# Banded attention on one core: scores normalised a unit ahead and head by head, biased scores placed between the pieces of the low parts

## The reference, cut to what matters

```python
def chunk_band_attention(qc, kb, vb, key_valid, rel_bias, offset):
    rel = offset + jnp.arange(nq)[:, None] - jnp.arange(nk)[None, :]
    bias = rel_bias[:, jnp.clip(rel, -REL_CLIP, REL_CLIP) + REL_CLIP]
    s = jnp.einsum('bnqhd,bnkhd->bnhqk', qc, kb) * (HEAD_DIM_B ** -0.5) + bias[None, None]
    s = jnp.where(key_valid[None, :, None, None, :], s, NEG)
    p = jax.nn.softmax(s, axis=-1)
    return jnp.einsum('bnhqk,bnkhd->bnqhd', p, vb)
```

## Time and profile before

| what | value |
|---|---|
| three timed runs | 1681.31, 1684.39 and 1684.91 us, median 1684.39 us |
| the profiled execution | 1680.23 us, of it a span of 1678.5 us, mean granted clock 0.973 |
| PE (matmuls) busy | 1585.2 us, 94% of the span |
| VectorE (DVE) busy | 1012.9 us, 60% |
| ScalarE (ACT) busy | 653.5 us, 39% |
| GpSimd (POOL) busy | 305.2 us, 18% |
| band stage | from about 395 us to 572 us of the span |

### The profile page before, as it was taken

The page is one execution under the profiler, slowest core; times in us unless marked ns, Lnnn a source line. Parts: engine busy times, 40 slices in busy tenths (PEclk is TensorE's granted clock), DMA queues, the critical chain, the costliest instruction groups (busy, mean ns, idle before and its releaser), DMA issues.

```text
span 1678.5 us, 27557 instructions
## 1 busy us (share of the span) xinstructions
PE 1585.2 (94%) x11172; PEld 1545.9 (92%) x11172; DVE 1012.9 (60%) x1481; ACT 653.5 (39%) x1146; POOL 305.2 (18%) x354
## 2 busy tenths in 40 slices
PE   6999999997888899999779999999999999999999
PEld 6999999995777799998669999999999999999999
DVE  6625876536888754225653477666666658656653
ACT  5521021126787632214552253333333433333332
POOL 1011000002221010000430004444444421010110
PEclk8999999987999999999999999999999999999999
DMA  7424111002110043201042214433334586454563
GB/s 241 143 89 159 50 39 38 26 1 92 36 37 33 26 138 138 89 26 51 1 148 100 90 55 152 147 143 141 142 142 166 202 281 235 123 165 147 155 211 114
DMA packets 63667, 189.36 MB, mean 113 GB/s; under 512 B 7873, under 2 KB 13049, under 8 KB 63409
## 3 DMA queue, kind: packets, MB, share of 16 engines
q1 hardware_dynamic: 37904, 91.11, 17.1%
q0 software_dynamic: 25648, 96.65, 16.0%
HBM read 138.58 MB, written 54.12 MB: 115 GB/s over the span
## 4 chain that ended last, share of the span: by engine, by line
PE 81%; DVE 7%; ACT 5%; DMA 4%; issue 3%; POOL 1%; SPq 0%; ACTq 0%; DVEq 0%; POOLq 0%
PE ps L452 33%; PE ps L2605 19%; PE ps L2626 17%; PE ps L2163 3%; PE ps L481 2%; DMA a<-wdn 2%; PE ps L2504 2%; PE ps L2356 1%; ACT scores L1168 1%; PE ps L2334 1%; DVE pt_lo L1759 1%; PE ps L2472 1%; PE ps L503 1%; PE ps L2318 1%; DVE scores L1738 1%
## 5 line engine op out<-in xcount | busy, mean ns | idle before, releaser
L452 PE MATMUL ps<-A_hi,w_hi 128*128 128x364 f32 x768 | 174.0, 335 | 0.0
L452 PE MATMUL ps<-A_lo,w_hi 128*128 128x364 f32 x768 | 171.1, 331 | 0.0
L452 PE MATMUL ps<-A_hi,w_lo 128*128 128x364 f32 x768 | 170.7, 331 | 0.0
L393 DVE TENSOR_TENSOR w_lo<-w_raw,w_hi 128x1024 fp32r<-128x1024 f32 x43 | 52.5, 1223 | 150.0 <-ACT w_hi L389 149.6
L389 ACT ACTIVATE w_hi<-w_raw 128x1024 fp32r<-128x1024 f32 x42 | 44.3, 1057 | 241.7 <-PE ps L452 136.2
L452 PEld LDWEIGHTS ps<-A_lo,w_hi 128*128 128x128 f32 x768 | 135.1, 190 | 0.0
L452 PEld LDWEIGHTS ps<-A_hi,w_lo 128*128 128x128 f32 x768 | 135.0, 190 | 0.0
L452 PEld LDWEIGHTS ps<-A_hi,w_hi 128*128 128x128 f32 x768 | 134.2, 191 | 0.0
L2605 PE MATMUL ps<-t_hi,wq_hi 128*128 128x272 f32 x480 | 99.9, 290 | 2.3 <-DVE hid_stage L2059 2.3
L2605 PE MATMUL ps<-t_lo,wq_hi 128*128 128x272 f32 x480 | 99.9, 290 | 0.0
L2605 PE MATMUL ps<-t_hi,wq_lo 128*128 128x272 f32 x480 | 99.7, 289 | 0.0
(11 more groups left out here) (342 smaller groups left out, 4087.6 us busy)
## 6 DMA issues: line engine op xcount, KB each, us to landing
w_raw<-slabs SPq DMA_DIRECT2D x68, 512.0 KB, 4.0
quads_d<-quad_sum POOLq DMA_DIRECT2D x64, 272.0 KB, 2.9
w_raw<-wdn POOLq DMA_DIRECT2D x32, 512.0 KB, 4.0
r_raw_a<-quads_d SPq DMA_DIRECT2D x56, 272.0 KB, 3.1
r_raw_b<-quads_d SPq DMA_DIRECT2D x56, 272.0 KB, 3.0
quads_d<-hid_stage POOLq DMA_DIRECT2D x48, 272.0 KB, 2.9
Y<-xT POOLq DMA_DIRECT2D x16, 546.0 KB, 4.6
y_d<-Y POOLq DMA_DIRECT2D x16, 546.0 KB, 3.2
```

Source lines behind the costliest of these rows:

```text
L393: e.tensor_tensor(WL[:, par], RAW[:, par], WH[:, par].bitcast(F32), ALU.subtract).then_inc(s.w_lo, 1)
L452: ins = e.matmul(PS[:, 3 * par + c, 0:CH], wt[:, wpar, w], xt[:, col:col + CH], start=(first and n == 0 and m == 0), stop=(last and n == l ...
```

## The change

Four orders and two waits are altered; the arithmetic is the same but that the two reciprocals of a unit, one instruction of two columns before, are two instructions of one column now. TensorE issues S(n+2) ahead of V(n-1). ScalarE runs E two units ahead, not one. VectorE does N(n+1) first, then the first two pieces of L(n), then B(n+2), then the rest of L(n).

```diff
                     if n >= 2:
-                        e.wait_ge(s.rec_done, n - 1)
+                        e.wait_ge(s.rec_done, 2 * n - 2)
...
             exps(0)
+            exps(1)
             for n in range(N_U):
                 pt_hi(n)
-                if n + 1 < N_U:
-                    exps(n + 1)
+                if n + 2 < N_U:
+                    exps(n + 2)
...
-                e.wait_ge(s.exp_done, 2 * n + 2)
-                if n >= 2:
-                    e.wait_ge(s.p_ready, 2 * n - 2)
-                e.reciprocal(REC[:, m:m + 2], SUM[:, m:m + 2]).then_inc(s.rec_done, 1)
-                e.wait_ge(s.rec_done, n + 1)
                 for h in range(2):
+                    e.wait_ge(s.exp_done, 2 * n + h + 1)
+                    if n >= 2:
+                        e.wait_ge(s.p_ready, 2 * n - 3 + h)
+                    e.reciprocal(REC[:, m + h:m + h + 1], SUM[:, m + h:m + h + 1]).then_inc(s.rec_done, 1)
+                    e.wait_ge(s.rec_done, 2 * n + h + 1)
...
             biased(0)
+            biased(1)
             normalise(0)
             for n in range(N_U):
                 if n + 1 < N_U:
-                    biased(n + 1)
-                pt_lo(n)
-                if n + 1 < N_U:
                     normalise(n + 1)
+                early = min(2, pieces(n))
+                pt_lo(n, range(early))
+                if n + 2 < N_U:
+                    biased(n + 2)
+                pt_lo(n, range(early, pieces(n)))
...
                 transposes(n)
+                if n + 2 < N_U:
+                    scores(n + 2)
...
                 if n:
                     values(n - 1)
-                if n + 2 < N_U:
-                    scores(n + 2)
```

More of the change, by code:

```diff
@@ L1745, in normalise, with pt_lo @@
                 m = 2 * (n % 2)
-                e.wait_ge(s.exp_done, 2 * n + 2)
-                if n >= 2:
-                    e.wait_ge(s.p_ready, 2 * n - 2)
-                e.reciprocal(REC[:, m:m + 2], SUM[:, m:m + 2]).then_inc(s.rec_done, 1)
-                e.wait_ge(s.rec_done, n + 1)
-                for h in range(2):
+                for h in range(2):
+                    e.wait_ge(s.exp_done, 2 * n + h + 1)
[3 more added lines that the diff above has]
+                    e.wait_ge(s.rec_done, 2 * n + h + 1)
                     e.tensor_scalar(SS[n % 2][:, h, 0:cols], SS[n % 2][:, h, 0:cols], REC[:, m + h:m + h + 1], None,
                                     ALU.mult).then_inc(s.p_ready, 1)
-            def pt_lo(n):
-                for p in range(pieces(n)):
+            def pt_lo(n, ps):
+                for p in ps:
                     rows, w = piece(n, p)
```

## The result

| | before | after |
|---|---|---|
| median of the runs | 1682.85 us (1681.21 to 1684.91, 4 runs) | 1744.28 us (1740.83 to 1747.64, 4 runs) |
| ratio | | 1.0367 (95% interval 1.0329 to 1.0406) |
| span of the profiled execution | 1678.5 us | 1739.7 us |
| band stage: start of T(0) to end of V(35) | 398.0 to 571.9, 174.0 us | 399.1 to 630.0, 230.9 us |
| first down-projection matmul (start of the last stage) | 1333.4 us | 1391.0 us |

The kernel became slower by 61.4 us. In the profiled executions the span grew by 61.2 us, and 57.0 of them lie in the band stage.

What follows compares the result with a forecast made beforehand. The band stage is bound by loops between engines, none full; the change closes a longer ring. Block terms +43.6 and clock +6 on 1680.2 us give 1729.8, or 1734.0 as median; 1732 was taken, range 1712 to 1748.

Steps and rivals of the forecast that it cites:

- the 6 for the clock: Chunk iterations: pauses of about 2 us lower TensorE's clock, B waits for S; half of the 0 to +12 bounds, +6 us.
- The ring: Band stage, five-tile units: H, two pieces of L, B, E and O form a closed loop across VectorE and ScalarE, 4.92 us.
- A stretch with one chunk: Band stage, one q or k chunk to the next: chunk, `heads_nrm`, N, L, B, E and O add to 6.67 us, now 4.76.
- The bare ring of 4.92 us: Plain five-tile unit without chunk: H to L 0.63, L 1.21, B to E 0.86, E and O 2.22 us.
- the 4.7 us that the text named as a sign of being wrong: Band stage: plain units repeating in under 4.7 us would show the prediction wrong, as would short ScalarE waits ahead of E.
- The sum: Growth of the four blocks of the band stage: 11.2, 12.6, 13.6 and 6.2, all in all +43.6 us.
- the term that was mis-sized: N in the chunk stretches: 1.33 us, being 1.13 from a profile row and 0.20 for a second reciprocal.
- the 3.6 of the sum: Last block: five iterations with ScalarE's extra 1.1 us, 6.0 us each against 5.35 now, together +3.6 us.
- The term's bound of 12: TensorE's clock falling in all 16 chunk iterations, +0.75 us each: upper bound +12 us; lower bound 0.
- The end of the stage: Band stage in the profile after: ends near 615 us, not 572.
- The reciprocals: VectorE's N: 36 extra one-column instructions, each costing between nothing and 0.20 us; 0.20 taken.
- The rival for which the page spoke: Band stage: ring not closed, waits of N for E and T for N go; -10 us, 1674; chance 0.05.

## Why the prediction was right, and where not

- **Direction and range.** Slower by over 0.2% had 0.91; 1744.3 lies in 1712 to 1748, 12 us above the value and 4 under the upper bound. In part that is luck: the two terms of the sum, 43.6 and 6, give 49.6 us, where the band stage grew by 57.0. Of the 6 for the clock about 2 were shown, and the 43.6 were too little by 13.
- **The ring.** H, two pieces of L, B, E, O: right, link by link. In the last block two B of head 0 start 6.05 us apart (605.74 and 611.79), worked out as 6.0. A stretch with one chunk took 6.67 us, worked out as 6.67. ScalarE's wait ahead of E was put at 1.2 to 1.5 us and is 2.0 on the mean (69.2 in 35 waits). The bare ring of 4.92 us occurs nowhere by itself: every turn has a chunk, an extra operation of ScalarE or a narrow unit in it. The nearest are T(16) to T(17) and T(25) to T(26), which took 5.03 and 4.64 us, with the B of a unit of one tile. The second is under the 4.7 us that the text named as a sign of being wrong; for that narrow B it says little.

```profile
605.74 0.82 DVE L1739 CUSTOM_DVE_ANT_0 scores<-ps,bias 128x640 f32<-128x640 f32 x1
...
611.79 0.81 DVE L1739 CUSTOM_DVE_ANT_0 scores<-ps,bias 128x640 f32<-128x640 f32 x1
```

- **The sum.** By blocks, growth measured and forecast:

| stretch | before | after | growth | forecast |
|---|---|---|---|---|
| T(0) to T(8) | 41.2 us | 57.1 us | 15.9 us | 11.2 us |
| T(8) to T(17) | 42.4 us | 59.3 us | 16.9 us | 12.6 us |
| T(17) to T(26) | 41.3 us | 59.3 us | 18.0 us | 13.6 us |
| T(26) to the end of V(35) | 49.1 us | 55.3 us | 6.2 us | 6.2 us |

The whole miss is in the three blocks with chunks. In the second one the stretches with more than 0.5 us too much are those with a long N (b = 2 to 3, 9.4 us for 8.0; 3 to 4, 8.8 for 7.3; 5 to 6, 8.7 for 8.0) and b = 1 to 2 (7.5 for 6.9), where S at the lower clock held B by 0.53 us. The others were worked out within 0.4 us (12.9 for 13.1, 6.7 for 6.7, 5.4 for 5.0). So the term that was mis-sized is N: it was priced from a row without GpSimd beside it (0.47 us a head), and the new order put N, now in the ring, right where q, k and cache are subtracted. Of the 13.4 us by which 43.6 fell short of 57.0, 7.5 are that by the run that moved GpSimd's work, and 2.1 the clock, for which the prediction had its own term. Where the last 4 or so come from stays open; the stretch from b = 2 to 3, which gained next to nothing from either run, is part of it. In the first block there is also a chunk wait of 5.51 us for the statistics at 426.75, behind cache copies and O. A slip in the last block changes little: five turns of 0.67 us are 3.4 us, not the 3.6 of the sum.
- **The clock.** The stage ran at 0.86, not 0.94, so falls did come; what keeping the clock up gave back was 2.1 us. The term's bound of 12 counted 16 iterations with chunks at 0.75 us each. There are 18, but B stood for S in only four of them, for 0.07 to 0.76 us, 1.8 us in all (the profile names no releaser there; by the order of the program it is S). At 0.91 the clock was not back to 0.94, so a small rest of this term is not tested.
- **The end of the stage** was forecast near 615 us and came at 630: the same mis-sized term in three blocks, and T(8) of the first block 17.0 us later, not 11.2.
- **The reciprocals** were priced at up to 0.20 us each; the rows of after have 0.16 busy and 0.19 to the next instruction. The 0.19 us show in the last block (5.35 to 5.54 us from T to T) and are lost in the scatter of the whole. The estimate of 0.06 us each by the table of the Trainium skill, page "VectorE: DVE Perf Modes", is further off than the row.
- **The rival for which the page spoke** (the Trainium skill, "Perfetto Trace Analysis", section "Optimizing Scalar/DVE Operations": breaking up instructions may let work finish sooner) gave no gain in the kernel with the cut reciprocals alone. There the wait of N for E went from 6.5 to 0.3 us, and the wait of T for N behind it stayed (10.4 and 10.5 us).
- **What I didn't see**: that S ahead of V would have cost about as much without the lead. I took that part for a plain help.

## What to carry to other kernels

Before an operation is run a unit ahead, write down the ring that it closes: for each engine, what is queued behind the moved operation, and whether that feeds the thing it waits for. Two things that are late together (O and the chunks here) can be better off ahead of an operation that depends on a third engine (24 us here while the ring was closed), and a producer that is asked for early must be issued ahead of every wait that isn't its own. An edit that is right beside one order can be a loss beside the other, so undo parts in pairs before a part is blamed.

## What the runs showed of the hardware

A multiplication by a column from SBUF to SBUF on VectorE takes 0.55 us for 640 columns alone. Beside a subtraction on GpSimd it took up to 2.08 us, and each of the twelve long ones ended 0.35 us after GpSimd's instruction, whether that one had 512 or 1092 columns. GpSimd's 1092 columns took 2.5 us either way. The operations of VectorE that read PSUM ran beside the same subtractions without growing (B 0.82 us, L 0.68 us a piece). With GpSimd's work moved, N came back to 33.35 us of 44.05.

A lower TensorE clock in a stage that is bound by waits between engines need not cost time: from b = 2 to 3 the granted clock behind the chunk was 0.69 or 1.00, and the stretch took 9.38 or 9.39 us.
